# Three taps a round in place of four in the long convolution beside the local attention

## The reference, cut to what matters

```python
z = x @ w_in
sc_b, sc_c, sc_h, q, k, v, cc_a, cc_gate = jnp.split(z, IN_OFFSETS, axis=-1)
y_sc = sc_b * depthwise_conv(sc_c * sc_h, sc_conv_w)          # 3 taps
q = rope(q...); k = rope(k...)
y_att = banded_window_attention(q, k, v, attn_sink)           # 8 heads of 64, 4 blocks of 128 queries
u = cc_a * jax.nn.sigmoid(cc_gate)                            # 256 columns
u = depthwise_conv(u, cc_conv_w) + cc_conv_b                  # 31 taps
y_cc = jax.nn.silu(layer_norm(u, cc_ln_g, cc_ln_b))
return jnp.concatenate([y_sc, y_att, y_cc], axis=-1) @ w_out
```

## Time and profile before

| | |
|---|---|
| median of 3 runs | 3388.27 us (3387.78 to 3392.65) |
| the profiled execution | 3390.67 us, of which its span is 3388.9 us |
| mean granted clock of TensorE | 0.996 of full speed |
| PE busy in the span | 3337.4 us (98%) |
| DVE, ACT busy | 1755.9 us (52%), 1313.8 us (39%) |
| the two mixers | about 378 to 572 us, and 1310 to 1506 us |

### The profile page before, as it was taken

How to read it: one execution, slowest core, us unless ns; L and a number is a source line. 1 busy time by engine, 2 the same in 40 slices (tenths; PEclk the granted TensorE clock), 3 DMA queues, 4 the chain that set the end, 5 groups by cost and what they waited for, 6 DMA issues and landing times.

```text
span 3388.9 us, 38104 instructions
## 1 busy us (share of the span) xinstructions
PE 3337.4 (98%) x15588; PEld 2749.6 (81%) x15588; DVE 1755.9 (52%) x2652; ACT 1313.8 (39%) x2091; POOL 70.3 (2%) x81
## 2 busy tenths in 40 slices
PE   9999999999999999999999999999999999999999
PEld 7888877888888888778888778877888789778887
DVE  5333785333453337853434875647444765655443
ACT  3222555322242225543322554434332465444232
POOL 0000100000000001000000000000000000000000
PEclk9999999999999999999999999999999999999999
DMA  5333411333333334113333333222333423223332
GB/s 160 99 94 90 91 50 56 112 99 94 94 93 96 97 90 91 50 56 109 109 94 93 94 100 101 87 63 84 101 98 97 84 63 100 68 62 108 94 99 69
DMA packets 650046, 304.11 MB, mean 90 GB/s; under 512 B 93456, under 2 KB 647568, under 8 KB 649744
## 3 DMA queue, kind: packets, MB, share of 16 engines
q1 hardware_dynamic: 649872, 301.66, 31.5%
HBM read 299.52 MB, written 2.10 MB: 89 GB/s over the span
## 4 chain that ended last, share of the span: by engine, by line
PE 86%; DVE 9%; ACT 4%; issue 1%; DMA 0%; SPq 0%; DVEq 0%; ACTq 0%
PE ps L1816 26%; PE ps L1824 26%; PE ps L1817 26%; DVE Y L2422 1%; DVE wl L2234 1%; PE ps L1891 1%; PE ps L1832 1%; PE ps L1876 1%; PE ps L1990 1%; PE ps L1974 1%; DVE XR L2345 1%; DVE XL L2331 1%; ACT XH L2059 1%; DVE M L2391 1%; ACT wh L2005 0%
## 5 line engine op out<-in xcount | busy, mean ns | idle before, releaser
L1824 PE MATMUL ps<-XL,wh 128*128 128x512 f32 (+1 forms) x2856 | 1062.1, 382 | 0.8 <-DVE XL L2323 0.8
L1816 PE MATMUL ps<-XH,wh 128*128 128x512 f32 (+1 forms) x2630 | 1044.8, 398 | 7.0 <-DVE wl L2234 3.7
L1817 PE MATMUL ps<-XH,wl 128*128 128x512 f32 (+1 forms) x2630 | 1019.1, 388 | 0.0
L2234 DVE TENSOR_TENSOR wl<-raw,wh 128x1024 fp32r<-128x1024 f32 (+1 forms) x565 | 681.8, 1209 | 470.9 <-ACT wh L2005 470.3
L2005 ACT ACTIVATE wh<-raw 128x1024 fp32r<-128x1024 f32 (+1 forms) x565 | 585.5, 1039 | 556.3 <-PE ps L1824 528.5
L1824 PEld LDWEIGHTS ps<-XL,wh 128*128 128x128 f32 x2856 | 538.4, 189 | 104.7 <-DVE XL L2323 1.8
L1816 PEld LDWEIGHTS ps<-XH,wh 128*128 128x128 f32 x2630 | 495.9, 189 | 121.6 <-ACT XH L2059 11.2
L1817 PEld LDWEIGHTS ps<-XH,wl 128*128 128x128 f32 x2630 | 496.3, 189 | 97.9 <-issue 1.9
L1816 PE MATMUL ps<-HHa,wh 128*128 128x512 f32 x1088 | 428.8, 394 | 5.8 <-DVE HLa L2238 5.8
L1817 PE MATMUL ps<-HHa,wl 128*128 128x512 f32 x1088 | 424.3, 390 | 0.0
L1824 PE MATMUL ps<-HLa,wh 128*128 128x512 f32 x1088 | 408.5, 390 | 0.0
(11 more groups left out here) (325 smaller groups left out, 2978.8 us busy)
## 6 DMA issues: line engine op xcount, KB each, us to landing
raw<-in_ffn_w_gu SPq DMA_DIRECT2D x176, 512.0 KB, 3.7
raw<-in_w_ff SPq DMA_DIRECT2D x128, 512.0 KB, 4.1
raw<-in_ffn_w_down SPq DMA_DIRECT2D x64, 512.0 KB, 3.9
raw<-in_w_xkv SPq DMA_DIRECT2D x32, 512.0 KB, 3.9
raw<-in_ev_w_in SPq DMA_DIRECT2D x25, 512.0 KB, 3.9
raw<-in_ffn_w_down SPq DMA_DIRECT2D x32, 384.0 KB, 3.4
raw<-in_w_in SPq DMA_DIRECT2D x22, 512.0 KB, 3.9
raw<-in_w_out SPq DMA_DIRECT2D x64, 128.0 KB, 2.8
```

What stands on the lines that cost most here:

```text
L1816: e.matmul(bank[:, c], t.wh[u % SPL][:, k, :], h[:, c], start=first, stop=False, skip_group_check=True)
L1817: e.matmul(bank[:, c], t.wl[u % SPL][:, k, :], h[:, c], start=False, stop=False, skip_group_check=True)
L1824: m = e.matmul(bank[:, 0:n], t.wh[u % SPL][:, k, :], l, start=False, stop=last, skip_group_check=True)
L2234: self.e.tensor_tensor(wl, raw, f32(wh), ALU.subtract).then_inc(self.s["lo"], self.tag("lo", f"lo.{i}"))
```

## The change

`long_conv` is written so that a round takes three taps: one of half 0, one of half 1, and a third that goes to the halves in turn. While only half 0 has begun, `min(i, len(gens) - 1)` gives all three to half 0. A half that has its 31 taps gives its turn to nobody. The attention's rounds, the filler's interval and all other lines are the same.

```diff
         def long_conv():
             while len(gens) < 1:
                 yield
-            n = [0, 0]
+            n, turn = [0, 0], 0
             while n != [31, 31]:
-                for _ in range(2):
-                    for i in range(len(gens)):
-                        if n[i] < 31:
-                            last[i] = next(gens[i])
-                            n[i] += 1
+                for i in (0, 1, turn % 2):
+                    i = min(i, len(gens) - 1)
+                    if n[i] < 31:
+                        last[i] = next(gens[i])
+                        n[i] += 1
+                turn += 1
                 yield
             st = Stats(self, True)
```

## The result

The changed kernel takes 3396.68 us in the median of 9 runs (3394.22 to 3399.56), the kernel before, on the same chip, 3389.37 us (9 runs, 3387.78 to 3392.65). The ratio is 1.0022 with a 95% interval of 1.0013 to 1.0031. The forecast was 3392.4 us in a range of 3382 to 3402: the time lies in the range, 4.3 us above the point, on the number that the prediction gave for the milder form of its first rival (3396). As a change against the kernel before, +4.1 us was forecast and +7.3 us came. The profiled execution took 3395.07 us, its span 3393.3 us.

The account below looks back on a forecast made before the run. The prediction took PE (TensorE), busy 98% of the span, as the bound. Its terms, 3.5 - 3.8 + 1.5 + 0.85 = +2.05 us a layer, +4.1 for both, put 3388.27 at 3392.4 us, range 3382 to 3402.

Parts of the forecast that it names:

- Rival 1: Drain ahead of hidden tiles 6 and 7 decides, slower: +6.7 us a layer, 3401 us; milder form 3396; chance 0.28.
- early loss: Rounds 1 to 12: extra taps make DVE late at the reciprocal of 456.70, +3.5 us a layer.
- rival 2: First rounds fit into DVE's idle time at 416 to 445: faster, -3.8 us a layer, 3381 us; chance 0.17.
- term 2: Rounds 13 to 25: DVE catches up and PE's waits for ACT's copy go, -3.8 us a layer.
- Term 3: Layer norm moves from the products of `w_in` into the drain: +6.1 - 4.6 = +1.5 us a layer.
- Term 4: Granted clock in the mixer: one drop goes, others come in the drain and first rounds, net +0.85 us a layer.
- (a): Value product's longest wait for ACT's copy within 45 us after first tap, 2 to 4 us; later 2.93 wait under 1.
- (b): PE's wait for the layer norm's sum is gone among the products of `w_in`.
- (c): Tile 6 starts 15 to 20 us behind `w_in`'s last product, tile 7 four later with a wait of about 2.
- (d): The granted clock falls in the drain and no longer at 490.
- Rival 3: Nothing binds where it moves: DVE's lateness is harmless and the lumps cancel, 3388 us; chance 0.06.
- Rival 4: ACT table switches in the drain cost twice what the trace shows: +5.5 us on the forecast, 3398 us; chance 0.05.

Follow-up runs that it names:

- third_to_half1: Changed kernel with the third tap of a round always to half 1, so that the taps end in round 25; 3391.03 us, before 3390.9.
- after_tile1_later: Changed kernel with out_project's hidden tiles in the order 0, 2, 3, 1, 6, 7, 4, 5; 3386.62 us, before 3391.2.
- last_taps_late: Kernel before with only the last five taps moved, into rounds 28 to 30, and the norm following them; 3400.09 us, before 3388.22.

## Why the prediction was near, and which step failed

*Terms 1 and 2, the early loss and the middle gain.* Each had its sign and nearly its size: +3.9 for +3.5, and -5.6 for -3.8. Their structure was wrong. They were taken as two quantities of which each could come out otherwise, and rival 2 (3381 us, 0.17) stood on that: a small loss early and the whole gain later. The traces show one meeting point instead, the value product at 490 us. It starts between 489.7 and 490.7 in ten of the twelve, whether PE has waited before or not (in the changed kernel it is just in time, 0.37 us behind the start of the matmul before). The others are `third_to_half1`, at 492.1, and `after_tile1_later`, at 493.4 in a layer that started 1.8 us late and had more low clock on the way. No rate of taps that was run came out measurably faster than before. The prediction had asked what is late next in this stretch and answered "nothing"; it was that same product. The 1.8 us by which term 2 was too small are mostly the refill of PE. Kernel before:

```profile
457.03 0.40 PE L1824 MATMUL ps<-XL,wh 128*128 128x512 f32 x1
...
458.63 0.60 PE L1876 MATMUL ps<-M 128*128 128x256 f32 x2
...
501.62 0.83 PE L1891 MATMUL ps<-Y,M 128*128 128x128 f32 x6
```

Without a wait the next matmul starts 0.23 us behind the start of such a one; with the wait of 0.42 us it started 0.83 us behind it (457.86), 0.60 more, and the six matmuls then took 0.77 us to the next group in place of 0.67 (501.62 to 502.29). So this wait costs 0.28 us more than the number in its brackets; those of 0.72 and 2.93 us come to 0.25 and 0.26 by the same reading. Four waits went (0.26, 0.33, 0.72 and 2.93): 4.24 + 4 x 0.28 = 5.4 of the 5.6 us.

*Term 3, the norm and the drain.* This is the step that failed: "Tiles 0 and 1 with their attention rounds take PE 5.8 us." They took 10.9 (510.10 to 521.0): 2.9 us of gap ahead of tile 1 (513.60 to 516.51), some 1.5 us of refill and low clock behind it, and 6.5 us for the tiles and rounds themselves, 0.7 more than the prediction had. The column sums start at +12.05 in place of +8.15. The 4.6 us of column sums had been PE's work, but also the time in which DVE made tile 1: its product stands at 514.39 where it stood at 517.11, 2.7 us earlier, while PE comes 6.2 us earlier. The row of before (DVE):

```profile
517.11 0.66 DVE L2253 TENSOR_TENSOR Y<-M,ps 128x512 f32<-128x512 f32 x1
```

The prediction took the block's 4.6 us as gained and did not ask who had used them; and it did not put the last taps, which by its own list came in rounds 28 to 30, ahead of tile 1's product on DVE. The other links of the chain were right: from the column sums to tile 6 it had 18.1 - 8.15 = 9.95 us, and measured 10.5. The drain's 10.1 us are: 3.0 for the moved column sums, 2.4 more in waits for tiles (5.30 for 2.88), 1.5 for the broadcast, 0.6 for two more refills and 3.4 for two stretches of low clock, 10.9 in all, of which some lies over waits.

*Term 4, the clock.* +0.85 a layer; the windows have 8.5 us in both layers for 5.1, so +1.7 a layer in the mean, all of it in the first. There are three windows there for one: behind the early wait, behind tile 1's wait and in tile 6. The rule was right in its place (the clock falls where PE has waited, at 461 in place of 490) and short by the wait that was not foreseen.

*The sum.* Its middle came near in part by luck: term 2 was 1.8 us a layer too small a gain, term 3 some 4 us too small a loss, and the two errors have opposite signs. The bounds are added up wrongly: as the terms state them they give -5.8 to +11.0 us a layer, not -5.6 to +13.35. The range was set inside both, so nothing hangs on it.

*The signs.* (a) right: 2.94 us at 461.87, and none between 465 and 510 (0.87 us in the second layer). (b) right. (c) wrong: 22.6 us in place of 15 to 20, and tile 7's wait 0.46 in place of 2, taken up by the slow tile 6. (d) right.

*The rivals.* Rival 1 named the place (ahead of tiles 6 and 7), the sign and the condition (tile 6 later than 20 us); it lacked the mechanism, since the chain's links had their forecast size and tile 1 was late. Its milder number, 3396, is the time measured, and with 1.0022 the kernel lies on the bound between "no change" and "slower". Rival 3 would have been right for the same taps ending in round 25. Rival 4 did not come: in the changed kernel the root starts 1.30 us behind the start of its table's load (526.42, 527.72), as in the earlier trace rows.

What stays open: why the granted clock falls more often when tile 1 waits. It accompanies the wait in all five kernels, but `third_to_half1` has 8.5 us of it without that wait and no loss in the median, and no run here took the clock away from the wait; how much of the loss is clock is therefore an estimate. And whether `last_taps_late` is slower than the changed kernel at all: by the ratios it is some 4 us, but the intervals overlap and the waits in the drain are nearly the same.

## What to carry to other kernels

Waits of the bound engine on one chain of another engine are not to be added: find the instruction at which they meet, and count only what moves that one. When a block of work is taken out from in front of an instruction, ask what else used the time, because it was cover for another engine's queue. And where a consumer can take its inputs in any order, put the one whose producer is last behind the others: here that was worth 9 us to the kernel with the late taps and 5 us to the kernel before, more than any way of spreading the producer's work.

## What the runs showed of the hardware

- A wait of TensorE costs 0.25 to 0.28 us beyond its bracket (three waits of the kernel before: 457.86, 483.65, 490.46): 0.15 to 0.18 us ahead of the next matmul, 0.10 for the first matmuls behind it.
- Filling TensorE's waits of 1.5 and 2.2 us with 128x256 matmuls did not keep the clock up: the low stretch came one tile later, and the kernel was no faster (1.0029 of before, 1.0022 without them).
- Stretches at the lower clock also come where nothing was changed: before has a window of 0.83 at 2030 us that none of the other eleven traces has, which makes single profiled executions differ by 1.7 us.
